# Who makes the rests of the feed-forward weights: VectorE for both matrices, or GpSimd for the first

## What is computed

```python
def sqrelu_mlp(x, w1, w2):
    h = jax.nn.relu(x @ w1)
    return (h * h) @ w2
...
h = h + sqrelu_mlp(rms_norm(h, norm_gain[layer, 1]), mlp_w1[layer], mlp_w2[layer])
```

## Time and profile before

| What | Value |
| --- | --- |
| median of 3 runs | 2541.74 us (2540.83 to 2543.3) |
| the profiled execution | 2541.81 us |
| its span in the trace | 2539.8 us |
| TensorE busy | 2377.6 us, 94% |
| VectorE busy | 1606.2 us, 63% |
| ScalarE busy | 1100.4 us, 43% |
| GpSimd busy | 754.0 us, 30% |
| granted TensorE clock, mean | 0.978 of full |

### The profile page before, as it was taken

One profiled execution on the slowest core, in us unless ns is written; L12 is line 12 of the kernel. 1 busy time (PEld: TensorE's weight loads), 2 busy tenths in 40 slices (PEclk: granted clock), 3 DMA queues, 4 the chain that ended last, 5 costly groups with the idle time before them and its releaser, 6 DMA issues.

```text
span 2539.8 us, 36841 instructions
## 1 busy us (share of the span) xinstructions
PE 2377.6 (94%) x13845; PEld 1890.6 (74%) x13845; DVE 1606.2 (63%) x2449; ACT 1100.4 (43%) x1986; POOL 754.0 (30%) x851
## 2 busy tenths in 40 slices
PE   7999899999999898999999799989999899899998
PEld 6777788777577665777877688879989797555555
DVE  3333277787564786487777666762067643588888
ACT  4444344444321575344445333341145401267776
POOL 7654400000007003400000644435742276411112
PEclk9999999999999899999999899999999999899999
DMA  4111223332323000332331211112210022389998
GB/s 136 53 56 50 80 79 117 116 89 78 104 88 99 18 1 7 111 83 83 116 116 43 71 51 43 46 55 67 83 42 26 26 92 87 134 290 366 362 364 300
DMA packets 267748, 268.46 MB, mean 106 GB/s; under 512 B 13258, under 2 KB 198437, under 8 KB 267603
## 3 DMA queue, kind: packets, MB, share of 16 engines
q1 hardware_dynamic: 263075, 254.04, 31.2%
q0 software_dynamic: 4528, 12.44, 1.9%
HBM read 256.24 MB, written 10.21 MB: 105 GB/s over the span
## 4 chain that ended last, share of the span: by engine, by line
PE 67%; DVE 16%; ACT 6%; DMA 5%; issue 5%; POOL 2%; SPq 0%; DVEq 0%; POOLq 0%; ACTq 0%
PE psum L2865 12%; PE psum L2868 12%; PE psum L2869 12%; DMA ex_tile<-in_w_down 5%; PE psum L1539 2%; PE psum L2503 2%; PE psum L2569 2%; ACT w_hi L2964 2%; PE psum L872 2%; PE psum L1254 2%; PE psum L874 2%; DVE w_lo L2982 2%; PE psum L873 2%; PE psum L1317 1%; PE psum L1309 1%
## 5 line engine op out<-in xcount | busy, mean ns | idle before, releaser
L2865 PE MATMUL psum<-x_hi,w_hi 128*128 128x264 f32 (+2 forms) x1560 | 527.2, 338 | 20.9 <-DVE x_lo L785 7.2
L2868 PE MATMUL psum<-x_lo,w_hi 128*128 128x264 f32 (+2 forms) x1560 | 517.9, 332 | 0.0
L824 POOL TENSOR_TENSOR w_hi<-ring_tile,one 128x256 fp32r<-128x256 f32 (+1 forms) x284 | 235.9, 858 | 461.0 <-PE psum L2869 429.5
L2869 PE MATMUL psum<-x_hi,ring_tile_lo 128*128 128x264 f32 (+2 forms) x1096 | 340.7, 311 | 0.0
L2865 PEld LDWEIGHTS psum<-x_hi,w_hi 128*128 128x128 f32 x1560 | 296.1, 190 | 55.9 <-issue 21.1
L2868 PEld LDWEIGHTS psum<-x_lo,w_hi 128*128 128x128 f32 x1560 | 296.3, 190 | 27.6 <-issue 1.2
L828 POOL TENSOR_TENSOR ring_tile_lo<-ring_tile,w_hi 128x256 fp32r<-128x256 f32 (+1 forms) x284 | 294.8, 1065 | 8.1
L2869 PEld LDWEIGHTS psum<-x_hi,ring_tile_lo 128*128 128x128 f32 x1096 | 208.1, 190 | 11.2
L2869 PE MATMUL psum<-x_hi,w_lo 128*128 128x512 f32 (+1 forms) x528 | 202.4, 383 | 0.0
L2865 PE MATMUL psum<-w_hi,hid_hi 128*128 128x512 f32 x448 | 176.4, 394 | 13.0 <-DVE w_lo L2982 13.0
L2964 ACT ACTIVATE w_hi<-ring_tile 128x1024 fp32r<-128x1024 f32 x128 | 130.8, 1050 | 123.2 <-PE psum L2869 112.5
(11 more groups left out here) (454 smaller groups left out, 5529.5 us busy)
## 6 DMA issues: line engine op xcount, KB each, us to landing
ring_tile<-in_mlp_w SPq DMA_DIRECT2D x128, 512.0 KB, 4.1
ex_tile<-in_w_gate SPq DMA_DIRECT2D x64, 512.0 KB, 12.4
ex_tile<-in_w_up SPq DMA_DIRECT2D x64, 512.0 KB, 12.0
ex_tile<-in_w_down SPq DMA_DIRECT2D x64, 512.0 KB, 12.0
ring_tile<-in_w_in SPq DMA_DIRECT2D x52, 512.0 KB, 3.8
ring_tile<-in_sb_w_qkv SPq DMA_DIRECT2D x24, 512.0 KB, 3.8
ring_tile<-in_nsa_w_kv SPq DMA_DIRECT2D x12, 512.0 KB, 3.8
ring_tile<-in_sb_w_o SPq DMA_DIRECT2D x8, 512.0 KB, 3.3
```

The costliest lines, as they stand in the source:

```text
L824: last = pool.tensor_tensor(hi[:, cols], raw[:, cols], one[:, :].broadcast_to([P, D // len(parts)]), ALU.mult)
L2865: upper = pe.matmul(dst, a_hi, b_hi, start=first, stop=False, skip_group_check=True)
L2868: pe.matmul(dst, a_hi, b_lo, start=False, stop=False, skip_group_check=True)
L2869: return pe.matmul(dst, a_lo, b_hi, start=False, stop=final, skip_group_check=True)
```

## The change

The rests of the first matrix's tiles (n = 0 to 7) go to GpSimd in every part; VectorE keeps those of the second matrix (n = 8 to 21) and, as before, all block sums. At a block's start `ff_pool` makes rests 2 and 3. In turn j = 0 to 3 it makes the rest of tile j + 4 and only then gives back slot j; in turn 14 it waits until all rests of the part are made, makes the next part's 0 and 1, in turn 15 its 2 and 3, and then gives back the slot of that turn. VectorE's `lower` leaves out n below 8 and from 22 on, and waits before n = 8 for the eight rests of GpSimd.

```diff
         def ff_pool(pool, m):
             read = [*range(FF_TILES), 10, 11, 16, 17, 16, 17, 20, 21]
+            for n in (2, 3):
+                ff_lower(pool, m, 0, n)
             for f in range(FF_PARTS):
                 for j in range(2 * FF_TILES):
+                    if j + SPLITS < FF_TILES:
+                        ff_lower(pool, m, f, j + SPLITS)
+                    elif j >= 2 * FF_TILES - 2 and f + 1 < FF_PARTS:
+                        pool.wait_ge(split_w, ff_no(m, f, FF_STREAM))
+                        for n in (0, 1) if j == 2 * FF_TILES - 2 else (2, 3):
+                            ff_lower(pool, m, f + 1, n)
                     pool.wait_ge(split_w, ff_no(m, f, read[j]) + 1)
...
         def ff_dve(dve, m, upd, leave=0):
 
             def lower(f, n):
-                if n < FF_STREAM:
+                if FF_TILES <= n < FF_STREAM:
+                    if n == FF_TILES:
+                        dve.wait_ge(split_w, ff_no(m, f, n))
                     ff_lower(dve, m, f, n)
-                elif f + 1 < FF_PARTS:
-                    ff_lower(dve, m, f + 1, n - FF_STREAM)
```

## The result

The changed kernel takes **2556.05 us** (median of 4 runs, 2555.11 to 2556.09), beside 2541.28 us for the kernel before in the same comparison (4 runs, 2537.25 to 2543.3). The ratio is 1.0054, with a 95% interval of 1.0043 to 1.0066: 0.54% slower. The prediction was 2551.4 us (+0.38%) with a range to 2554.5. So the direction was right and the size was not: the time lies 1.5 us outside the range. The profiled execution of after took 2555.11 us, its span 2553.0, against 2541.81 and 2539.8 before: 13.2 us of span to be accounted for. One of the ten runs of a kernel further down (the next part's tiles) took 4295 us at a mean granted clock of 0.795, and the ratios leave it out.

The account below looks back on a forecast made before the run. It took VectorE's chain through the hidden tiles to product 2, where TensorE idles once a part, as the bound. Sums' collisions 5.6 us plus `x_lo` 4.0 made 9.6 on 2541.81: 2551.4 us, range 2546.0 to 2554.5.

Parts of the forecast that it names:

- What bounds the kernel: Ahead of product 2, TensorE idles 1.63 us a part; when VectorE gets through the hidden tiles counts, not how much it does.
- The floor under the removal's gain: Hidden tile 5's square can't start before its relu ends; removal alone gives at most 0.28 us a part, about 2 us.
- No other slack: Behind hidden tile 5, the order on VectorE and ScalarE stays as before, with no further slack to be had.
- The collision in hidden tile 3: GpSimd's rest holds up VectorE's second block sum; `hid_hi` starts 0.70 us later, 8 x 0.70 = 5.6 us.
- The last `x_lo` of each block: At block starts GpSimd's rest 2 issues 0.03 us ahead and delays VectorE's last `x_lo`: 2.2 + 1.8 = 4.0 us.
- The rival "sums only": Only the block sums are held up, the last `x_lo` slips through: 2547.4 us, slower by 0.22%; chance 0.23.
- The clock: At product 2 the forecast counted TensorE's idle time as 2.3 us and had no term for the granted clock.
- The fourth rival, "more is held up": First `hid_lo` of hidden tile 3 also collides, or GpSimd rests run longer: up to 0.5 us more a part, 2555.5; chance 0.06.
- The engines hinder each other: VectorE instructions with two SBUF inputs don't run beside GpSimd; the second sum takes about 2.5 us in hidden tiles 1 and 3.
- The rival without hindrance: The engines don't hinder each other at these instructions; the removal alone counts, 8 x 0.28 = 2 us less, 2539.6; chance 0.12.

Follow-up runs that it names:

- next tiles: Changed kernel with only the rests of the next part's tiles 0 to 3 and the block starts on GpSimd, 4 to 7 on VectorE: 2541.63 us, 1.0.
- rest 7 given back: Changed kernel with tile 7's rest made by VectorE again in hidden tile 3, GpSimd keeping 0 to 6: 2541.06 us, 1.0004.
- held back: Changed kernel with GpSimd's rests in hidden tiles 1 and 3 waiting for the pair's last `hid_lo`, so behind the sums: 2539.21 us, 0.9996.
- five with 0.61 or less: Sums before rests: 2532.97 us; plus rests held back on GpSimd: 2532.94; `turn` of tile 13 moved: 2539.26; sums and `turn`: 2528.93; all three: 2528.31.
- half dose: Kernel before plus one unread VectorE maximum over 350 columns in hidden tile 3 of each part, no rests moved to GpSimd: 2550.54 us, 1.0036.
- full dose: Kernel before plus one unread VectorE maximum over 700 columns in hidden tile 3 of each part, no rests moved to GpSimd: 2552.75 us, 1.005.
- own tiles: Changed kernel with only the rests of tiles 4 to 7 of each part on GpSimd, 0 to 3 on VectorE: 2551.49 us, 1.0043.
- `x_lo` held: Changed kernel plus one GpSimd subtraction at each block's start, let go while VectorE has one `x_lo` left: 2555.25 us, 1.0057.
- the sums first: Kernel before with VectorE's sums put ahead of the rest in the odd hidden tiles, no work moved between engines: 2532.97 us, 0.9966.

## Why the prediction was wrong in its size

All runs at product 2, eight parts each:

| Kernels | Idle, us a part | Parts with half clock behind it |
|---|---|---|
| before; next tiles only | 1.63 | 0 of 16 |
| rest 7 given back | 1.69 | 0 of 8 |
| held back (1.38), and five with 0.61 or less | up to 1.38 | 0 of 48 |
| half dose | 2.06 | 3 of 8 |
| after; full dose; own tiles; `x_lo` held | 2.41 to 2.42 | 4, 4, 4 and 2 of 8 |

Step by step:

- **What bounds the kernel** was right: of the rests moved, only those that shift the start of product 2 show in the time.
- **The floor under the removal's gain** was right: at most 0.28 us a part, 0.25 measured with the rests held back. "No other slack" holds for the old order alone; with the sums first, 0.78 us more are found behind tile 5.
- **The collision in hidden tile 3** was right in place and kind: `hid_hi` 0.70 us late by the sum, 0.72 by the trace. At TensorE it came to 0.79 a part, 6.3 us and not 5.6. Giving back the one rest removed it, and so did letting it start later.
- **The last `x_lo` of each block** is a step of the sum that failed: 4.0 us foretold, 0 measured. The prediction took the earlier trace rows, where GpSimd issued 0.03 us ahead and VectorE had to wait. Here GpSimd was 26 ns ahead and had to wait itself. The cost if it does go first was nearly right, 3.4 us. The Trainium skill (SBUF — State Buffer, Who interferes with whom) lets the one that issues first have the access; by the trace's time stamps agrees and the block starts don't. Other rows show that so small a lead tells nothing. With the changed kernel and the five others that have GpSimd make rest 2 there (next tiles, rest 7 given back, held back, and the two with the sums first as well), the near tie comes 12 times, GpSimd 21 to 32 ns ahead; VectorE went first 12 times, with the third `x_lo` still running. And the line of the earlier trace rows has, in the same trace of before, four cases in which VectorE issued 15 to 21 ns ahead and yet had to wait, with a GpSimd subtraction already running. One of them, on VectorE and GpSimd:

```profile
1888.67 1.32 DVE L2096 SCALAR_TENSOR_TENSOR norm<-raw,head_gain,sq 128x528 f32<-128x528 f32 x1
...
1887.11 3.48 POOL L828 TENSOR_TENSOR ring_tile_lo<-ring_tile,w_hi 128x256 fp32r<-128x256 f32 x4
```

GpSimd's row is four subtractions back to back. In both cases the engine already at work went on. But with `x_lo` held, GpSimd had issued 0.44 us ahead of the fourth `x_lo` and got in between the third and the fourth, so what decides stays open. The rival "sums only" had 0 for this term, and gave 2547.4.

- **The clock** is the step that made the forecast too low: a term that is missing altogether. The sum counted 2.3 us of idle time for TensorE as 2.3 us. But idle time has a price beyond its length: behind 2.42 us the granted clock was half for 3.4 us in half of the parts, 4 x 1.55 = 6.2 us. It was shown without GpSimd. Nothing in the trace of before told of it at this place, where the clock is full behind 1.63 us; other stages of it do have half-clock stretches (836.4 to 843.0 us, granted clock 0.50), and the prediction looked at none of them. With this term and without that of `x_lo` the sum on the profiled execution's own time is 2541.8 + 6.3 + 6.2 = 2554.3 (profiled: 2555.1). The two errors, 4.0 too much and 6.2 + 0.7 too little, cancel in part and leave 2.9 us; that the forecast comes as near as it does is luck. The fourth rival, "more is held up" (2555.5), is nearest in time and wrong in its reason: the first `hid_lo` of hidden tile 3 took 0.69 us and GpSimd's rests 2.40 at the median, as ever.
- **The engines hinder each other** was the question on which the sign hung, and the earlier trace rows answered it: the second sum takes 2.50 us in two tiles of four. The rival without hindrance fell.

What remains: 0.7 us of span, and that the median of after lies 0.9 us above its profiled execution. In the attention stages both kernels have half-clock stretches that come at slightly different places in each run, and I put it down to them without having shown it. Why a given part gets the half clock stays open too.

## What to carry to other kernels

Before work is moved from VectorE to an idle GpSimd, look at which VectorE instructions with two SBUF inputs will run beside it, and whether one of them is on the path: here one collision of 2 us a part turned a small gain into a loss, and waiting for the sums' end cured it. Try first what the order of work within VectorE gives: putting the four sums ahead of an instruction whose result is needed later was worth 8 us, four times what moving 60 instructions gave at best. And when a change lengthens an idle stretch of TensorE, price not only its length but also the clock behind it.

## What the runs showed of the hardware

- TensorE's granted clock fell to half for one stretch of 3.4 us at 17 of 40 places with 2.06 to 2.42 us of idle time, between 0.5 us before the end of that idle time and 1.1 us behind it, and at none of 72 places with 1.70 us or less, with the same dense matmuls on both sides. One such stretch costs 1.55 us. Which of the places it takes differs between kernels with the same 2.42 us.
- A VectorE instruction with two SBUF inputs and a GpSimd subtraction shut each other out in either direction: 0.42 us became 2.50 (GpSimd ahead), and 2.40 became 2.96 (VectorE ahead). At a near tie the time stamps don't tell which goes first: GpSimd lost 12 times with 21 to 32 ns of lead, won with 32 ns, and won four times in that trace with VectorE 15 to 21 ns ahead.
